# Second mixer of a two-block transformer: modulation sums ahead of the first gate pair, softmax ahead of the older step's transposes, ten of sixteen gate units split

## The reference

```python
mod = silu(c) @ w_ada + b_ada            # 6 parts: shift, scale, gate for mixer and feed-forward
h = rms_norm(x, g_pre_mix) * (1.0 + sc_m) + sh_m
z = h @ w_in + b_in
q, k, v, glu_a, glu_b, gate_a, gate_b = split(z)      # 512 x5, 1024 x2
a = chunked_rel_attention(q, k, v, rel_bias) @ w_attn_o
u = causal_dwconv(glu_a * sigmoid(glu_b), w_dw, b_dw)  # 31 taps
u = silu(layer_norm(u, g_ln, b_ln))
cb = u @ w_conv_o + b_conv_o
y = sigmoid(gate_a) * a + sigmoid(gate_b) * cb
x = x + gt_m * rms_norm(y @ w_mix_o, g_post_mix)
# then a feed-forward with a 3-tap conv, modulated by the other three parts
```

## Time and profile before

| | before |
|---|---|
| median of 3 runs | 819.17 us (818.78 to 820.41) |
| profiled execution, its own time | 818.51 us |
| span of the profiled execution | 816.7 us |
| TensorE busy, share of the span | 781.8 us, 96% |
| VectorE busy | 577.8 us, 71% |
| ScalarE busy | 389.9 us, 48% |
| GpSimd busy | 29.4 us, 4% |
| mean granted TensorE clock | 0.995 of full |
| second mixer's matmuls, from the first glu unit to the first conv-output matmul | 425.7 to 578.8 us |

### The profile page before, as it was taken

The page is one execution under the profiler, slowest core; times in us unless marked ns, Lnnn a source line. Parts: engine busy times, 40 slices in busy tenths (PEclk is TensorE's granted clock), DMA queues, the critical chain, the costliest instruction groups (busy, mean ns, idle before and its releaser), DMA issues.

```text
span 816.7 us, 13601 instructions
## 1 busy us (share of the span) xinstructions
PE 781.8 (96%) x5424; PEld 716.9 (88%) x5424; DVE 577.8 (71%) x959; ACT 389.9 (48%) x656; POOL 29.4 (4%) x36
## 2 busy tenths in 40 slices
PE   7999999988999999999998999999999999999997
PEld 6987999876799999999977988788978999999995
DVE  5847767676675876768665988565878667677676
ACT  5562332543453534434473534337358555565554
POOL 0020000002000000000011100000000000000000
PEclk9999999999999999999999999999999999999999
DMA  6732133475259988789714632444653455655541
GB/s 252 264 128 78 55 102 113 146 233 187 98 188 392 346 289 287 267 286 344 271 49 155 204 114 70 129 129 145 195 202 95 168 202 165 205 172 191 197 130 52
DMA packets 40527, 148.96 MB, mean 182 GB/s; under 512 B 4496, under 2 KB 4624, under 8 KB 40080
## 3 DMA queue, kind: packets, MB, share of 16 engines
q1 hardware_dynamic: 39456, 142.62, 51.1%
q10 hardware_dynamic: 1008, 5.47, 1.7%
HBM read 147.02 MB, written 1.05 MB: 181 GB/s over the span
## 4 chain that ended last, share of the span: by engine, by line
PE 67%; DVE 12%; issue 9%; ACT 7%; POOL 2%; DMA 2%; DVEq 0%; POOLq 0%; ACTq 0%
PE bank L932 12%; PE bank L935 12%; PE bank L933 12%; PE bank L949 6%; PE bank L959 5%; PE bank L957 5%; PE bank L960 5%; PE bank L1088 4%; DVE wlo L1313 4%; DVE arena L1319 2%; ACT whi L1824 2%; ACT XN L1824 2%; POOL small L2138 2%; DVE arena L1313 2%; ACT arena L1824 1%
## 5 line engine op out<-in xcount | busy, mean ns | idle before, releaser
L932 PE MATMUL bank<-hh,whi 128*128 128x256 f32 x1024 | 293.5, 287 | 6.8 <-DVE small L1313 4.0
L933 PE MATMUL bank<-hl,whi 128*128 128x256 f32 x1024 | 290.4, 284 | 0.0
L935 PE MATMUL bank<-hh,wlo 128*128 128x256 f32 x1024 | 290.3, 284 | 0.0
L1313 DVE TENSOR_TENSOR wlo<-raw,whi 128x1024 fp32r<-128x1024 f32 x204 | 243.7, 1230 | 43.7 <-ACT whi L1824 43.3
L1824 ACT ACTIVATE whi<-raw 128x1024 fp32r<-128x1024 f32 x204 | 204.0, 1047 | 31.3 <-DMA raw<-w_dram 17.6
L932 PEld LDWEIGHTS bank<-hh,whi 128*128 128x128 f32 x1024 | 196.7, 192 | 12.2 <-issue 4.6
L933 PEld LDWEIGHTS bank<-hl,whi 128*128 128x128 f32 x1024 | 196.8, 192 | 1.5
L935 PEld LDWEIGHTS bank<-hh,wlo 128*128 128x128 f32 x1024 | 196.7, 192 | 0.0
L1319 DVE SCALAR_TENSOR_TENSOR arena<-bank,cols,arena 128x255 f32<-128x255 f32 (+3 forms) x138 | 58.9, 480 | 28.3 <-ACT arena L1824 26.8
L1824 ACT ACTIVATE arena<-bank 128x256 f32<-128x256 f32 (+2 forms) x65 | 26.7, 420 | 106.8 <-PE bank L935 72.0
L959 PE MATMUL bank<-wlo,fh 128*128 128x512 f32 x176 | 69.1, 392 | 0.4 <-DVE wlo L1313 0.4
(11 more groups left out here) (159 smaller groups left out, 879.3 us busy)
## 6 DMA issues: line engine op xcount, KB each, us to landing
raw<-w_dram SPq DMA_DIRECT2D x268, 512.0 KB, 4.7
arena<-rows_dram ACTq DMA_DIRECT2D x1, 1792.0 KB, 9.2
X<-x_dram SPq DMA_DIRECT2D x2, 512.0 KB, 4.5
arena<-rows_dram ACTq DMA_DIRECT2D x1, 1024.0 KB, 12.7
arena<-bias_dram ACTq DMA_DIRECT2D x1, 1024.0 KB, 15.9
out_dram<-X SPq DMA_DIRECT2D x4, 256.0 KB, 2.0
const<-const_dram ACTq DMA_DIRECT2D x1, 640.0 KB, 8.0
arena<-bias_dram ACTq DMA_DIRECT2D x1, 512.0 KB, 10.2
```

The source lines that it names most:

```text
L932: e.matmul(o, a, hh[:, k, :], start=(k == 0), stop=False)
L933: e.matmul(o, a, hl[:, k, :], start=False, stop=False)
L935: ins = e.matmul(o, wlo[:, s, k * 128:k * 128 + 128], hh[:, k, :], start=False, stop=(k == 7))
L1313: return e.tensor_tensor(out, a, b, op)
```

## The change

It has five parts. `mod_sum(1)` moves ahead of the first two glu pairs. In `attention2`, `soft2(n)` stands in the same turn as `turn2(n-1)` and no longer in the next one; `keep(15)` ahead of `turn2(0)` goes, and a `yield` stands in its place for n == 1. The gate pairs 1, 3, 5, 6 and 7, ten units, become of kind "s". In `conv31` two more turns lie between `mean` and `variance`. Last, `h_read_by[3]`, the moment from which `hh` may be written over, is now that of the last split gate unit.

```diff
+SPLIT_GATES = (1, 3, 5, 6, 7)
...
-    units += [("n", "w_in_2", 20 + n + 8 * m) for n in range(8) for m in range(2)]
+    units += [("s" if n in SPLIT_GATES else "n", "w_in_2", 20 + n + 8 * m) for n in range(8) for m in range(2)]
...
+    P.step("mod_sum", 1)
     first_four(2, ("glu0", "glu1"), "w_in_2", (12, 16, 13, 17))
     P.side = [4, 5, 6, 7]
-    P.step("mod_sum", 1)
...
-            yield from pair(f"gg{n}", "w_in_2", (20 + n, 28 + n), ("h", 2), "n")
+            yield from pair(f"gg{n}", "w_in_2", (20 + n, 28 + n), ("h", 2), "s" if n in SPLIT_GATES else "n")
...
         P.fill("mu")
         P.step("mean")
         yield
+        yield
+        yield
         P.fill("var")
...
             yield
+            if n == 1:
+                yield
             if n:
-                if n == 1:
-                    P.keep(15)
                 P.fill(f"pt2{n - 1}", frees=1)
                 P.step("turn2", n - 1)
-            yield
             if n < 8:
                 P.step("soft2", n)
+            yield
...
-        h_read_by = {1: last_of("w_in_z", 3), 2: last_of("w_gate_up", 2 * FT - 1), 3: last_of("w_in_2", 7)}
+        h_read_by = {1: last_of("w_in_z", 3), 2: last_of("w_gate_up", 2 * FT - 1), 3: last_of("w_in_2", 28 + SPLIT_GATES[-1])}
```

## The result

The kernel after takes 813.95 us, the median of 4 runs (812.63 to 815.43), against 819.79 us (818.78 to 820.50) for the one before on the same chip. The ratio is 0.9932, with a 95% interval of 0.9913 to 0.9951: faster by 5.8 us. Two executions of later kernels took far longer than the others of the same kernel (859.35 us with the sums alone, 1931.67 us with other banks) and are left out of every median, range and ratio. The profiled execution is the slowest of the four, 815.43 us.

The account below looks back on a forecast made before the run. TensorE was taken as the bound, the engine that waits least. Savings of 16.8 us, less new waits of 2.6, 2.0, 2.8 and 1.6, gave -7.8 us: 819.17 to 811.4 us, range 807.4 to 815.5.

Parts of the forecast that it names:

- second rival: Gate rounds for steps 2 to 7: each waits a further 0.5 to 1 us; 813 to 817 us, chance 0.18.
- Sums ahead: Second glu pair: moving the modulation sums removes the idle time and the half clock behind it, -5.65 us.
- Softmax ahead: Attention step 0: the filler and idle time around the transposes go, with real work in their place, -4.24 us.
- new wait at the values of step 0: Attention step 0: TensorE waits for ScalarE's copy of the transposes, which stands behind exponentials and a hi part, +2.6 us.
- Ten split units: Gate units: a split unit takes 2.88 us of TensorE instead of 3.38 us in plain fp32; ten give -5.0 us.
- Old waits that go: Variance and attention output: waits of 1.14 us for ScalarE's squares and 0.8 us in the tail go, -1.95 us.
- Values of step 1: Attention step 1: the same chain through VectorE and ScalarE makes TensorE wait again, +2.0 us.
- Mean: Ahead of the mean: TensorE waits for VectorE's last tap, with one split unit as cover, +2.8 us.
- Tail: Behind the mean: either one clock fall or the third attention-output unit waiting for its lo part, +1.6 us.
- the waits are absorbed: Rival: of 9.0 us of new waits only 4 to 6 stay and no clock falls; 806 to 809 us, chance 0.20.
- The first edit does nothing: Rival at the second glu pair: another wait replaces the modulation sums, stall and clock stay; 817.1 us, chance 0.03.
- Slower: Rival at the ten split units: TensorE waits over 0.8 us more at each; 826 us at 1.5 us each, chance 0.04.

Follow-up runs that it names:

- other banks: The kernel after with the second and third attention-output unit in banks 6 and 7 in place of 1 and 0: 811.70 us.
- the mean later: The kernel after with two more turns between the last tap and the mean: 809.57 us.
- u later: The kernel after with two more turns between the variance and the activation of u: 814.37 us.

## Why the prediction was right, and where it was off

Predicted were 811.4 us with a range of 807.4 to 815.5; the median is 813.95. It lies in the range, but above the likeliest case (809 to 813 us). The prediction had its second rival there (VectorE behind at every gate round), and those waits did not come; what made the time longer is mostly the tail. That the range reached so far up for another reason is luck. By its own steps:

- **Sums ahead, -5.65.** Right: 5.74 us of mixer's length when done alone. No loss that the rows show.
- **Softmax ahead, -4.24**, and **new wait at the values of step 0, 2.6.** Both right in place and size: no filler, no wait at the transposes, 2.69 us behind. By itself the edit changes nothing that can be measured (819.57 against 819.09). What stands behind the idle time is the order in ScalarE's queue: the run with the copy ahead of the exponentials has neither wait.
- **Ten split units, -5.0.** Right as a term (5.56 us in the pair of runs with and without). The Trainium skill's figures ("FP8 and Floating Point Precision", TensorE Precision Notes; "TensorE: Matmul & The Clock Gate", Back-to-back issue gap) gave 8.7 us as an estimate, by a formula that the page states for an isolated matmul; the runs are nearer to the rows. That the splits only pay with cover is shown from both sides: alone they cost 3.3 us, and six more of them cost 6.4.
- **Old waits that go, -1.95.** The wait at the variance is gone. The 0.8 us of the tail was not won: longer waits came there, below.
- **Values of step 1, 2.0.** 1.79 us. The prediction lets the clock fall behind the first wait and be absorbed by this one, and so it came with the mean later (0.30 us left here). In the profiled execution of after it fell behind this wait instead, 1.7 us (0.92 of full from 489 to 492 us and 0.63 from 492 to 496), and nothing absorbed it: the kernel with other banks has the same instructions up to the mean, no fall here and the same 2.48 us at the mean, and its mean starts 545.55 - 426.73 = 118.82 us behind the first glu matmul, 1.65 earlier than the 120.47 of after. Predicted was 545.2 - 425.66 = 119.54, so after is 0.93 us late there, and without the fall it would be 0.7 early.
- **Mean, 2.8.** 2.48 us, released by the last tap.
- **Tail, 1.6: the term that was mis-sized.** The prediction took either one clock fall or a wait for the third attention-output unit's lo part, and said that they exclude each other. What came was a wait of the second unit for its bank, 3.38 us, and a clock fall of 1.7 us behind it: 5.1 us where 1.6 were booked. From the mean to the first conv-output matmul it is 28.78 us, where 571 - 545.2 = 25.8 was predicted, 3.0 us more, so the work itself took about 0.5 us less than reckoned. I had asked when the unit's data come and not when its bank is free. With other banks the wait that I had reckoned with, for the third unit's lo part, is there, 0.44 us.

Together 0.93 + 3.0 = 3.9 us, which is 149.25 - (153.13 - 7.8). Of the profiled execution's 815.43 - 810.7 = 4.7 us the remaining 0.8 us lies ahead of the mixer, where before and after have the same instructions. These are windows of the kernel after and of the kernel before there:

```profile
168.00:171.00 3.00, 3.00 (x17) 3.00 (x17) 1.02 (x3) 1.70 (x3) 0.49 (x1) 0.55 0.51 199
```

```profile
168.00:171.00 3.00, 3.00 (x27) 3.00 (x27) 1.29 (x5) 1.72 (x3) 1.01 (x1) 1.00 0.50 202
```

One execution had a clock fall at 168 us and the other had none. Such falls in the first block come and go between executions of the same instructions, so where kernels are compared by single profiled executions the mixer's length is the safer measure. The median of after is 1.5 us under its profiled execution, and so 2.5 us above the prediction.

**The rivals.** That the waits are absorbed: no, 10.3 us of idle time and 3.4 us of clock stand in the mixer of the profiled execution, where the prediction booked 9.0 for both. VectorE behind at every gate round: not with ten units (no idle time of TensorE over 0.25 us between 491.45 and 546.97), but with sixteen it is late at some of them, and TensorE waits 3.25, 0.80 and 2.31 us at scores. The first edit does nothing: no. Slower: no. The sum of the savings, 16.8 us, was nearly right too: the fastest kernel has all the edits of the change, three more that take away the waits these opened, and one wait of 1.30 us; its mixer is 153.13 - 136.82 = 16.3 us shorter.

## What to carry to other kernels

When a stall is removed, list for the next consumer each thing that it waits for: data, and the buffer or bank that it writes to. The one that holds the bank can be an operation that was ready long ago and stands behind unrelated work in another engine's queue. Try first to move that operation ahead in its queue: the copy ahead of the exponentials took 3.25 us out of the mixer, while putting the values later brought nothing. Putting the mean later did pay, since the taps that it waits for are not put off with it. And weigh an edit together with its cover: each of two edits that save 4 to 5 us by their rows was worth nothing or less by itself.

## What the runs showed of the hardware

The clock falls behind some idle times of TensorE and not behind others of the same length at the same place. Behind 2.7 us at the values of step 0 it stayed at 1.00 in the kernel after and fell to 0.50 in the kernel with u later, which has the same instructions up to there; behind 2.48 us at the mean it stayed up in the kernel after and was 0.51 with other banks. It fell behind 1.79 us at the values of step 1 in the kernel after, and stayed at 1.00 behind the same wait with other banks. The Trainium skill's advice against idle gaps between bursts of matmuls ("TensorE: Matmul & The Clock Gate", Why this matters for your kernels) holds in the sense that every fall in the mixer stood behind one; the runs show no length below which one is safe. A fall costs 1.6 to 1.7 us most times. It cost 3.4 us at the mean of the kernel with the splits alone, and as much at the values of step 0 of the kernel with u later (0.69, 0.50 and 0.67 of full in three windows from 480 to 489 us). So taking a wait away can bring more than the wait: with other banks the mixer has 2.95 us less idle time than after's and is 4.43 us shorter.
